# A fused model kernel: the second model's queries and keys by feature, their rotation by shuffle and on GpSimd

## Time and profile before

| | |
|---|---|
| median of 3 runs | 1642.34 us (1642.09 to 1642.69) |
| the profiled execution, its own time | 1642.05 us |
| its span, first to last instruction | 1640.3 us |
| TensorE busy | 1627.6 us |
| VectorE busy | 1181.6 us |
| ScalarE busy | 981.5 us |
| GpSimd busy | 184.5 us, nothing in stages b0 and b1 |
| granted TensorE clock | 0.999 of full speed |

### The profile page before, as it was taken

The page is one execution under the profiler, slowest core; times in us unless marked ns, Lnnn a source line. Parts: engine busy times, 40 slices in busy tenths (PEclk is TensorE's granted clock), DMA queues, the critical chain, the costliest instruction groups (busy, mean ns, idle before and its releaser), DMA issues.

```text
span 1640.3 us, 27310 instructions
## 1 busy us (share of the span) xinstructions
PE 1627.6 (99%) x11138; PEld 1409.5 (86%) x11138; DVE 1181.6 (72%) x1655; ACT 981.5 (60%) x1521; POOL 184.5 (11%) x193
## 2 busy tenths in 40 slices
PE   9999999999999999999999999999999999999998
PEld 7989999988888999999988888778888887788886
DVE  7987447699888974547898885767756657667654
ACT  7684525565567675345555575666774556657743
POOL 0663400000002945100000000000000000000000
PEclk9999999999999999999999999999999999999999
DMA  7443534455545425525465555345345553444452
GB/s 284 164 155 112 191 104 145 164 194 196 185 169 201 159 99 168 162 99 185 140 223 194 186 193 188 129 153 172 137 165 177 188 202 131 153 158 151 145 189 77
DMA packets 48893, 270.12 MB, mean 165 GB/s; under 512 B 13632, under 2 KB 14656, under 8 KB 17024
## 3 DMA queue, kind: packets, MB, share of 16 engines
q1 hardware_dynamic: 38448, 265.22, 46.4%
q10 hardware_dynamic: 9712, 2.62, 0.7%
q0 software_dynamic: 608, 0.53, 0.2%
HBM read 266.51 MB, written 1.84 MB: 164 GB/s over the span
## 4 chain that ended last, share of the span: by engine, by line
PE 82%; DVE 12%; ACT 3%; issue 2%; DMA 1%; SPq 0%; DVEq 0%; ACTq 0%
PE bank L1792 15%; PE bank L1793 15%; PE bank L1797 15%; PE bank L1684 7%; PE bank L1729 5%; PE bank L1730 5%; PE bank L1734 5%; DVE w_low L1057 4%; PE bank L1689 3%; PE bank L2837 2%; ACT w_high L620 1%; ACT arena L721 1%; DVE arena L1256 1%; PE bank L2825 1%; PE bank L2869 1%
## 5 line engine op out<-in xcount | busy, mean ns | idle before, releaser
L1057 DVE TENSOR_TENSOR w_low<-slab,w_high 128x2048 fp32r<-128x2048 f32 (+1 forms) x249 | 571.9, 2305 | 209.1 <-ACT w_high L620 201.8
L620 ACT ACTIVATE w_high<-slab 128x2048 fp32r<-128x2048 f32 (+1 forms) x249 | 470.7, 1897 | 107.1 <-PE bank L1797 89.2
L1792 PE MATMUL bank<-w_high,act 128*128 128x512 f32 x1120 | 444.2, 397 | 1.4 <-DVE act L1220 0.7
L1793 PE MATMUL bank<-w_high,act 128*128 128x512 f32 x1120 | 436.9, 390 | 0.0
L1797 PE MATMUL bank<-w_low,act 128*128 128x512 f32 x1120 | 309.5, 389 | 0.0
L1729 PE MATMUL bank<-act,w_high 128*128 128x256 f32 x1024 | 258.6, 290 | 0.0
L1792 PEld LDWEIGHTS bank<-w_high,act 128*128 128x128 f32 x1120 | 210.4, 188 | 48.8 <-issue 7.5
L1730 PE MATMUL bank<-act,w_high 128*128 128x256 f32 x1024 | 251.7, 283 | 0.0
L1797 PEld LDWEIGHTS bank<-w_low,act 128*128 128x128 f32 x1120 | 210.2, 188 | 44.4
L1793 PEld LDWEIGHTS bank<-w_high,act 128*128 128x128 f32 x1120 | 210.6, 188 | 40.9
L1729 PEld LDWEIGHTS bank<-act,w_high 128*128 128x128 f32 x1024 | 195.8, 191 | 8.3 <-issue 5.6
(11 more groups left out here) (263 smaller groups left out, 1836.3 us busy)
## 6 DMA issues: line engine op xcount, KB each, us to landing
slab<-stream_a SPq DMA_DIRECT2D x143, 1024.0 KB, 4.9
slab<-stream_b SPq DMA_DIRECT2D x104, 1024.0 KB, 4.9
arena<-x_t SPq DMA_DIRECT2D x4, 256.0 KB, 7.0
slab<-stream_a ACTq DMA_DIRECT2D x2, 512.0 KB, 6.3
residual<-x_tok SPq DMA_DIRECT2D x1, 1024.0 KB, 10.9
lora_weights<-lora SPq DMA_DIRECT2D x2, 512.0 KB, 7.5
lora_weights<-final_rows SPq DMA_DIRECT2D x2, 512.0 KB, 5.8
d_inverse<-arena ACTq DMA_DIRECT2D x2, 256.0 KB, 2.3
```

The source lines that it names most:

```text
L620: line.did(eng.activation(core.wh[u % PARTS][:, 0:SLAB_WIDTH[u]], core.slab[u % SLABS][:, 0:SLAB_WIDTH[u]], ACT.Copy), core.sem("slab_high"))
L1057: line.did(line.eng.tensor_tensor(core.wl[u % PARTS][:, 0:SLAB_WIDTH[u]], core.slab[u % SLABS][:, 0:SLAB_WIDTH[u]], core.wh[u % PARTS][:, ...
L1792: eng.matmul(out, core.xh[:, at, columns_], wh[:, k, :], start=first and k == 0, stop=False, skip_group_check=True)
L1793: eng.matmul(out, core.xl[:, at, columns_], wh[:, k, :], start=False, stop=False, skip_group_check=True)
```

## The change

Slabs of queries and keys are cut by feature: one holds two tiles of 128 features for all 1024 inputs. `feature_pair` (TensorE) makes them as `up` does, one bank per tile. ScalarE copies the right half of each bank, VectorE adds it (`turned`) and writes, by one `stream_shuffle` of 512 columns for both tiles, a copy in which features 0..7 and 8..15 of each group of 32 partitions have changed places. GpSimd (`pool_b`) multiplies the copy by a table of sines, the pair by one of cosines, and adds. The tables are 128x256 each, by feature and token, loaded for each layer; `scale_row` multiplies them by the norm's scale of the token, which `pe_spread` has spread to all partitions (cosine 1 where nothing is rotated, sine 0). `qk_turn` is gone on TensorE and ScalarE; scores read the tiles directly, after a wait for GpSimd. Banks of these units are freed by VectorE. The core of the diff:

```diff
+TURNED = ("q", "k", "Q", "K")
...
-        elif i % 2 == 0:
-            product += 1
-            reader = "dve" if kind in ("pa", "pb") else "act"
+        elif kind in TURNED or i % 2 == 0:
+            product += 2 if kind in TURNED else 1
+            reader = "dve" if kind in TURNED + ("pa", "pb") else "act"
...
-            for name, lag in (("qk_turn", 0), ("turned" if late else "turn", 2), ("scores", 1), ("pv", 3), ("combine", 1)):
+            put(UNITS_B[host + n], ROUND_NEXT)
+            for name, lag in (("turned" if late else "turn", 2), ("scores", 1), ("pv", 3), ("combine", 1)):
                 if name == "combine":
                     put(UNITS_B[host + n], SPLIT_NEXT)
                 if 0 <= n - lag < 8:
                     put(UNITS_B[host + n], (name, 8 * kind + n - lag))
-                if name == "qk_turn":
-                    put(UNITS_B[host + n], ROUND_NEXT)
...
-    put(("v", 2), ("lam", 0))
+    put(("v", 2), ("lam", 0), ("scale_row", 0))
...
+            eng.dma_start(flat(core, BCOS_, 2), d["turns"]).then_inc(sem("model_in").sem, 16)
+            eng.wait_ge(sem("roped").sem, START["b1"]["roped"])
+            eng.dma_start(flat(core, BCOS_, 2), d["turns"]).then_inc(sem("model_in").sem, 16)
...
+def pool_b(core, eng, line, stage):
+    rows, sem, did = PLAN_B, core.sem, line.did
+    tt = eng.tensor_tensor
+
+    def unit(u):
+        kind, i = rows[u][0:2]
+        if kind not in TURNED:
+            return
+        pair, swapped = (x.rearrange("p (n t) -> p n t", n=2) for x in (turned_pair(core, kind, i), swapped_pair(core, u)))
+        eng.wait_ge(*sem("qk_swapped").next(eng))
+        did(tt(swapped, swapped, over(flat(core, BSIN_), 2), ALU.mult))
+        did(tt(pair, pair, over(flat(core, BCOS_), 2), ALU.mult))
+        line.settled()
+        did(tt(pair, pair, swapped, ALU.add), sem("roped"))
+
+    walk(SCHEDULE[stage], dict(unit=unit))
...
+def turned_tile(core, k, keys_):
+
+    return flat(core, BQK_[k // 4 % 2] + 4 * keys_ + k % 4)
...
+def turned_before(kind, i):
+
+    return 4 * (2 * kind.isupper() + i // 2) + 2 * (kind in "kK") + i % 2
...
+        if kind in TURNED:
+            for j in range(2):
+                made(core, eng, rows, u, j)
+                act(rest_of(core, u, j), bank[banks[j][0]][:, T:2 * T], ACT.Copy, sem("rest_copied"))
+            return
...
-        if kind in ("q", "k", "Q", "K"):
-            block = 2 * second + i // 2
-            if block >= 2:
-                sem("qk_turned").at_least(eng, 4 * block - 4)
-            for m in range(2):
-                made(core, eng, rows, u, m)
-                b = banks[m][0]
-                act(staged(core, kind, i, m), bank[b][:], ACT.Copy, sem(f"act_emptied{b}"), scale=token_scale(core, m))
...
-    def qk_turn(k):
-        eng.wait_ge(*sem("qk_turned").next(eng))
-        if k >= 2:
-            sem("scored").at_least(eng, k - 1)
-        act(turned_qk(core, k), bank[7][:], ACT.Copy, sem("act_emptied7"))
...
-    def rope(kind, i, banks):
-
-        spare = flat(core, BROPE_, 2).rearrange("p (m n h d) -> p m n h d", m=2, n=2, h=8)
-        for m in range(2):
-            table = lambda name: over(core.const(name, 32, CB)[:, 16 * m:16 * m + 16], 8)
-            b, _, n = banks[m]
-            dst = staged(core, kind, i, m).rearrange("p (h d) -> p h d", h=8)
-            src, crossed, straight = dst[:, :, 0:16], spare[:, m, 0], spare[:, m, 1]
-            eng.wait_ge(*sem(f"act_emptied{b}").upto(n))
-            did(tt(crossed, src, table("sin"), ALU.mult))
-            did(tt(straight, src, table("cos"), ALU.mult))
-            line.settled()
-            did(tt(dst[:, :, 0:8], straight[:, :, 0:8], crossed[:, :, 8:16], ALU.add))
-            did(tt(dst[:, :, 8:16], straight[:, :, 8:16], crossed[:, :, 0:8], ALU.add), sem("roped"))
+    def scale_row(_):
+        eng.wait_ge(sem("model_in").sem, 64 + 16 * layer)
+        eng.wait_ge(*sem("norm_spread").next(eng))
+        for at in (BCOS_, BSIN_):
+            did(tt(flat(core, at), bank[7][:, 0:T], flat(core, at), ALU.mult), sem("dve_emptied7") if at == BSIN_ else None)
+
+    def turned(u):
+        kind, i, _, _, banks = rows[u]
+        pair, swapped, before = turned_pair(core, kind, i), swapped_pair(core, u), turned_before(kind, i)
+        if before >= 8 and before % 4 < 2:
+            sem("scored").at_least(eng, before // 4 * 4 - 4)
+        for j in range(2):
+            b = banks[j][0]
+            eng.wait_ge(*sem("rest_copied").next(eng))
+            did(tt(pair[:, j * T:j * T + T], bank[b][:, 0:T], rest_of(core, u, j), ALU.add), sem(f"dve_emptied{b}"))
+        if before >= 2:
+            sem("roped").at_least(eng, before - 1)
+        line.settled()
+        did(eng.stream_shuffle(swapped, pair, [d ^ 8 if d < 16 else d for d in range(32)]), sem("qk_swapped"))
...
+    def feature_pair(u):
+
+        fills = rows[u][4]
+        eng.wait_ge(sem("slab_high").sem, first + u + 1)
+        wh, wl = (w[(first + u) % PARTS][:].rearrange("p (k j m) -> p k j m", k=KD, j=2) for w in (core.wh, core.wl))
+        for j in range(2):
+            b, reader, _ = fills[j]
+            banks.fill(b, reader)
+            out_ = core.bank[b]
+            for k in range(KD):
+                mm(out_[:].rearrange("p (n t) -> p n t", n=2), wh[:, k, j, :], core.x[:, :, k, :], start=k == 0, stop=False,
+                   skip_group_check=True)
+            if j == 0:
+                eng.wait_ge(sem("slab_split").sem, first + u + 1)
+            for k in range(KD):
+                last = mm(out_[:, 0:T], wl[:, k, j, :], core.xh[:, k, :], start=False, stop=k == KD - 1, skip_group_check=True)
+            last.then_inc(sem("products").sem, 1)
...
-    def qk_turn(k):
-        kind, i = ("q", "Q")[k // 8], 2 * (k % 8 // 4)
-        eng.wait_ge(*sem("roped").upto(4 * (k // 4) + 4))
-        banks.fill(7, "act")
-        qk_turn.at[k] = banks.count[7, "act"]
-        for n, name in enumerate((kind, "kK"[k // 8])):
-            for m in range(2):
-                ins = eng.transpose(bank[7][:, n * T + m * P:][:, 0:P], staged(core, name, i, m)[:, P * (k % 4):][:, 0:P],
-                                    core.const("ident"))
-        ins.then_inc(sem("qk_turned").sem, 1)
-    qk_turn.at = {}
+    def scale_row(_):
+        pe_spread(core, eng, banks, "dve_emptied7", 1)
 
     def scores(k):
-        eng.wait_ge(sem("act_emptied7").sem, qk_turn.at[k])
+        kind, i = ("q", "Q")[k // 8], k % 8 // 2
+        eng.wait_ge(*sem("roped").upto(turned_before(kind, i) + 3))
         banks.fill_pair(3, "dve")
-        qk = turned_qk(core, k)
+        queries, keys_ = turned_tile(core, k, 0), turned_tile(core, k, 1)
         for m in range(2):
             for p in range(2):
                 rows_ = slice(HD * p, HD * p + HD)
-                ins = mm(core.pair[:, p * BLOCK:][:, SPAN[m]], qk[rows_, m * P:m * P + P], qk[rows_, T:T + WIDTH[m]],
+                ins = mm(core.pair[:, p * BLOCK:][:, SPAN[m]], queries[rows_, m * P:m * P + P], keys_[rows_, 0:WIDTH[m]],
                          start=True, stop=True, skip_group_check=True)
```

More of the change, by code:

```diff
@@ L2388, in pool_program @@
     line.did(eng.memset(flat(core, IDLE_, 2), 0.0), core.sem("idle_set"))
-    for stage in ("a0", "a1"):
+    for stage in STAGES[:-1]:
         core.enter(stage)
-        pool_a(core, eng, line, stage)
+        (pool_a if stage[0] == "a" else pool_b)(core, eng, line, stage)
 def by_token(core, at, m):
@@ L2570, in scalar_b @@
     walk(SCHEDULE[stage], dict(root_table=lambda _: act_root_table(core, line), round=act_round(core, line, FIRST_SLAB[stage]), scaled=scaled, x_turn=scaled, square=square, norm=norm, lam=lam, unit=unit,
-                       qk_turn=qk_turn, scores=scores, turn=turn, turned=turn, pv=pv, silu=silu, rms=rms, post=post, gate=gate,
+                       scores=scores, turn=turn, turned=turn, pv=pv, silu=silu, rms=rms, post=post, gate=gate,
                        merge=merge))
@@ L2604, in norm @@
             line.tell(sem("tokens_scaled"))
+        dve_spread(core, line, scale)
     def lam_product(_):
@@ L2636, in unit @@
         banks = rows[u - 1][4]
-        if kind in ("q", "k", "Q", "K"):
-            if (stage, kind, i) == ("b0", "q", 1):
-                eng.wait_ge(sem("model_in").sem, 48)
-            rope(kind, i, banks)
-        elif kind in ("pa", "pb"):
+        if kind in ("pa", "pb"):
             if i == 1:
@@ L2746, in merge @@
         line.tell(sem("merged_low"))
-    walk(SCHEDULE[stage], dict(add=dve_add(core, line, stage), multiply=dve_multiply(core, line), split=dve_split(core, line, FIRST_SLAB[stage]), scaled=scaled, x_turn=scaled, norm=norm, lam_product=lam_product, lam=lam, unit=unit,
+    walk(SCHEDULE[stage], dict(add=dve_add(core, line, stage), multiply=dve_multiply(core, line), split=dve_split(core, line, FIRST_SLAB[stage]), scaled=scaled, x_turn=scaled, norm=norm, lam_product=lam_product, lam=lam, scale_row=scale_row, unit=unit,
```

(19 more changed lines are left out.)

35 lines of the change are left out of this document (21 added, 14 removed).

## The result

The changed kernel takes 1662.16 us (median of 4 runs, 1661.39 to 1662.97) against 1642.45 us (1642.09 to 1642.69) for the kernel before in the same comparison. The ratio is 1.0120, with a 95% interval of 1.0105 to 1.0135: 19.7 us slower. The forecast was 1651 us, with a range up to 1659.

The account below looks back on a forecast made before the run. TensorE was taken as the bound end to end, with VectorE's loop beside it having little room. From 1642.05 us, -1.6 (TensorE and VectorE) and +10.1 (GpSimd) gave 1650.6, with 0.3 for the median say 1651; range 1636 to 1659.

Parts of the forecast that it names:

- The direction and the place: Whole kernel: slower, chance 0.65; TensorE waits for VectorE's `combine` before share turns, 1 to 2.5 us behind k2 and k3.
- the 8.42 less 0.44 of the forecast: First attention's loop: TensorE's own step loses four transposes, 0.44 us, and becomes 7.98 us.
- TensorE's sum of 8.8 us: TensorE: transposes removed 14.1 us, dearer query and key units 4.5, spreading the scale 0.8; 8.8 us saved if nothing else moved.
- VectorE's term: Attention loops: additions and shuffle lengthen VectorE's steps, leaving a net gain of 1.6 us in two layers before GpSimd.
- rival 1: Attention loops: GpSimd and VectorE don't shut each other out, so only -1.6 us: 1640.7 us; chance 0.15.
- about 0.9 us per step: Loop steps with q3, k2, k3: one GpSimd blocking delays VectorE 0.9 us, twelve times, less 0.7 room: +10.1 us.
- the first attention's room of 0.35: First attention's loop: `combine` ends at 22.5, TensorE is ready at 22.8; 0.35 us absorbs delay first, twice.
- rival 3: Query and key units: GpSimd is the bound, VectorE's shuffles wait for the rotation; about 1659 us; chance 0.15.
- The bound of 2.1 us per step: Loop steps with query and key units: at most two GpSimd blockings, 1.04 + 1.04 us each step, giving 24.5 us.
- Rival 2: Attention loops: VectorE's work fits beside TensorE, which remains the bound; 8.8 us saved, 1633.5 us; chance 0.2.

## Why the prediction was half right

**The direction and the place were right.** TensorE's waits stand in front of the turns of the shares, in the three steps that share the loop with query and key units, in both attentions and both layers, and behind them only the second attention's weight loads wait, for some 0.4 us at a turn. The first attention's later steps are 7.98 us apart (1055.83, 1063.81, 1071.79 in the changed kernel), the 8.42 less 0.44 of the forecast. A feature unit takes the 5.58 us that the earlier trace rows gave. TensorE's sum of 8.8 us was somewhat too high all the same: it is busy for 6.1 us less without GpSimd's work (clock 0.998), and where the clock was 0.999 as before, 6.8 less with writes only (1620.8) and 5.7 less in the shifted order (1621.4 against 1627.1). The transposes are part of that: 32 more sets made TensorE busy for 13.1 us more (1640.7 against 1627.6), not 14.1. The rest isn't assigned.

**VectorE's term was near.** Without GpSimd's work the forecast was rival 1's 1640.7; the run gives 1644.24. The shuffle took 0.75 us, not 0.65, and the masking started 1.95 us after unit q3, not 1.7. Turn 2 came 23.2 us after it, not 22.8, turn 10 23.9 after Q3, not 23.5: 0.8 a layer, 1.6 in all. The other 2 us aren't assigned; that kernel's executions with a clock of 0.999 took 1642.3 to 1642.5, those at 0.996 and 0.997 took 1645.6 and 1646.4.

**The step that failed is GpSimd's: "about 0.9 us per step", twelve times, 10.1 us.** It measured 17.9, and these 7.8 us with the 3.5 of VectorE's term are the distance from 1651 to 1662. The step without arrears was sized well: 0.88, of which 0.63 is the wait of `combine` behind GpSimd's third operation that the forecast described, and 0.27 the negation's. But I gave it to all twelve steps. In the first step of each attention GpSimd still has the unit before, and the excess is 3.1 us (second attention) and 2.6 (first, 8.3 against 5.74). Summed over a layer from the steps' own lengths: 3.1 + 0.9 + 0.9 in the second attention, 2.6 + 1.0 + 1.1 in the first (6.77 against 5.74, 7.16 against 6.08), 9.7 before rounding; two layers 19.4, less the first attention's room of 0.35 twice, 18.7. The runs that took the arrears away put 5.9 us on them.

The arrears come from two numbers in rival 3's argument, "3.1 + 2.3 = 5.4" against a unit of 5.58. GpSimd's operation alone takes 1.29 us here, not the 1.04 of the earlier trace rows, for a reason that no run tells, and a blocked one 3.3. So 3.3 + 1.3 + 1.3 = 5.9 per unit, over 5.58, and from unit to unit GpSimd falls behind until the loop's longer steps let it catch up. A margin of 3% was argued on a price taken from another stage. Rival 3's place was right, its mechanism not quite: VectorE stands idle ahead of its shuffles for only 0.3 us in 32 of them; it is the exclusion that grows, because a GpSimd that isn't idle meets one operation of `combine` after the other.

**The bound of 2.1 us per step was no bound.** It let two operations block. With more waits in one step (negation, L2721, L2724, L2727), VectorE lost 3.1. And the upper end of the range, 1659, was rival 3's time, though the sum with that bound of 24.5 us gives 1665, which would have held the result.

**Rival 2** was far off in this order of the work, but it names what the change can do: with the loop moved behind the units, what came of the 8.8 us of TensorE was 3.4, in the traces 5.7 of busy time less 2.5 of waits that TensorE still has for `combine`.

## What to carry to other kernels

Work handed to an idle GpSimd isn't free when VectorE's row decides: here each operation of GpSimd that reads SBUF could hold up a two-input or a `TENSOR_SCALAR` operation of VectorE until it ended, however short that one is; the reciprocal and the maxima weren't held. Count how many GpSimd operations fall into the critical stretch, the ones in arrears among them, and compare GpSimd's time per unit with blockings included against the unit's period; a quotient near 1 is no margin: 5.4 us against 5.58 in the forecast was 5.9 in the run. If the work can be placed outside VectorE's loop, move the loop as well, and with it what shares its function tables and banks.

## What was not expected of the hardware

- A VectorE operation on 4 elements per partition (the negation L2703, 0.17 us alone) takes up to 0.99 us and one on 2 elements (L2721) 0.84 in place of 0.23, since they wait for the end of a GpSimd operation. The reciprocal on 4 elements (L2709) took 0.18 in all 16 rows, also beside GpSimd. The maxima just ahead (L2701, `TENSOR_REDUCE`) kept their 1.01 us for two in every row read.
- In the rows of the step with arrears the two engines take turns: L2721, L2724 and L2727 each waited behind one of GpSimd's operations, and the four short operations in a row (L2724 and L2727, two each) lost 2.0 us to two of them.
- Six settings to zero on GpSimd in place of the three operations, which read nothing, cost no time, but the negation still took 0.60 and 0.59 us twice in twelve steps.
- A shuffle of 512 columns took 0.75 us, more than an addition of two operands of the same size (0.69), and loading its mask 0.01.
- After a wait of 3.79 us TensorE's granted clock fell, and the next 16 products took 1.6 us longer.
